# Both column halves of the first pointwise product walked in one pass over the depth, modulation units reordered

## The chip, the cores and the metric

The kernel runs on one core of one Trainium2 chip. The time is that of the device for one launch, in microseconds (us); the median of three runs of the kernel before is 1011.45 us (1011.24 to 1011.48).

## What is computed

Two transformer-like blocks run one after the other on 256 tokens of width 1024, in fp32. The change lies wholly in the first half of the first block:

```
mod  = silu(c) @ w_mod + b_mod                 # six vectors of 1024: scale1, shift1, gate1, scale2, shift2, gate2
hl   = rms_norm(x, norm1_g) * (1 + scale1) + shift1
u    = hl @ w_pw1 + b_pw1                      # 1024 -> 2048: halves a and gate
u    = a * sigmoid(gate)
u    = depthwise_conv(u, width 31, segments of 64) + b_dw
u    = silu(layer_norm(u))
x    = x + gate1 * (u @ w_pw2 + b_pw2)
x    = x + gate2 * (relu((rms_norm(x, norm2_g) * (1 + scale2) + shift2) @ mlp_w1) ** 2 @ mlp_w2)
```

What follows (attention of three kinds, a gated MLP, an embedding gate, twice) isn't touched.

## The kernel before

**Weights as a stream.** All weights lie in HBM in the order in which they are used, cut into units of 1 MB (128 partitions x 2048 floats). `plan_units` (L85) writes this order out by hand. SyncE (SP) issues one DMA for each unit, in that order (`weights`, L508). In the first block a unit goes to the slot "its index modulo 6" (L166, `EARLY_SLOTS`), and its DMA waits until whoever reads the unit six places earlier has finished with it: for a split unit until its low part is made (`lo_done`), for a modulation unit until VectorE's dot products (`dot_done`) or TensorE's products (`mod_used`) are done. All of SP's work is one queue in program order, the small transfers among it.

**Split units.** A product in full precision takes three fp32r passes: ScalarE (ACT) copies a weight unit to its high part (`feed` of ACT, L626, at L635), VectorE (DVE) subtracts to get the low part (`feed` of DVE, L1087, at L1101), and TensorE (PE) does high x high, high x low and low x high (`three`, L1707, at L1713). There are three buffers for split parts; the high part of unit s waits until PE has done unit s-3 (`used`).

**The first pointwise product (pw1).** 1024 inputs are four depth groups of 256 (`GROUPS`, two k-tiles of 128 each); 2048 outputs are two column halves c = 0, 1, each for 512 columns of a and 512 of gate. So pw1 is eight units, named (c, i) here. `pw1_part` (L1841) does one k-tile or two of one unit for one token block b: 6 matmuls a k-tile, 24 a unit with both blocks. PE does all of c = 0 first, in four groups, and c = 1 behind it (L1917 to L1952). Before group i its input must be scaled and shifted by modulation: the scale columns come from a dot product on DVE (`dots`, L1161, two instructions a unit), the shift columns from PE (`quarters`, L1810, 8 matmuls and then `column_sums`, L1822, with a copy by ACT between, `quarter_copy`, L688). `group_input` (L1204) on DVE and `group_high` (L699) on ACT make the full, high and low parts of the input.

**Modulation units.** mod(v, q) is quarter q of vector v: v = 0 scale1, 1 shift1, 2 gate1, 3 shift2, 4 scale2, 5 gate2. Those in `DOTS` (L82) go to DVE, at 2 x 1024 elements a unit; the eight others go to PE. The units before, by index: mod00, pw1(0,0), mod10, then mod0i, mod1i, pw1(0,i) for i = 1 to 3, pw1(1,0) to (1,2), mod20, pw1(1,3), pw2(0), mod21, mod22, pw2(1), mod23, mod40, mod30, mod41, mod31, mod42, pw2(2), mod32, pw2(3), mod43, mod33.

**The convolution.** It is done as a product with fixed waves: `gates` (ACT, sigmoid, L707), `gated` (DVE, L1246), `modes` (PE, L1866), `filtered` (DVE, L1252), `tokens` (PE, L1874), `statistics` and `variance` (DVE), a small power on GpSimd, then ACT and DVE normalise one token block each (L749, L1308), `normal_T` (PE, L1886) transposes, `pair_of` (ACT, L757) applies silu and `low_pair` (DVE, L1313) makes the low part.

**Second pointwise product and residual.** pw2 is four units. DVE has the low parts of pw2(2) and pw2(3), dot products between them, and then `mid_residual` (L1343), which needs gate1 in rows: `gate_column(0)` (DVE, L1283) makes it from the dot products of mod20 to mod23, SP writes it to HBM (`gate_write`, L540, waits for `gate_done`) and reads it back broadcast (`gate_read`, L545). In SP's order:

```python
            end = units_of("pw2")[2]["index"]
            weights(UNITS[at:end])
            gate_write(0)
            at, end = end, units_of("pw2")[3]["index"] + 1
            weights(UNITS[at:end])
            gate_read(0, one["g1"])
```

In ACT's order of the kernel before, the high parts of pw2(0) and pw2(1) stand ahead of the sigmoids of c = 1 (L741 to L743), and a one-element Silu (L745) loads the next activation table.

Of the kernel before, what the change touches and what calls it, by code (L numbers as in the profile page):

```python
# [41 lines left out]
HD = 5  # L42
# [39 lines left out]
DOTS = {(0, 0), (0, 1), (0, 2), (0, 3), (2, 0), (2, 1), (2, 2), (2, 3), (4, 2), (3, 2), (4, 3), (3, 3), (5, 0), (5, 1), (5, 2), (5, 3)}  # L82


def plan_units():  # L85
# [34 lines left out]
    mod(2, 1, 2)  # L120
    pw2(1)
    mod(2, 3)
    mod(4, 0)
    mod(3, 0)
    mod(4, 1)
    mod(3, 1)
# [60 lines left out]
LOW_IN_TWO = [u["s"] for u in SPLIT if (u["stage"][0], u["n"], u["part"]) in (("mla", 0, 1), ("sb", 0, 0), ("gu", 0, 1), ("gate", 0, 3))]  # L187

MOD_BANKS = [5] * GROUPS + [7, 6, 2, 3]
SUM_AT = [(6, 0)] * GROUPS + [(3, QUARTER)] + [(6, 0)]  # L190
COLUMN_UNITS = ((None, 0), (None, 1), (None, 2), (None, 3), (4, 5), (6, 7))
# [46 lines left out]
def build(nc, stream, x, p_t, vectors, rows, rel, consts, dft_tables, taps, tap_bias, out):  # L238

    ctx = ExitStack()  # L240
    with ctx:
# [146 lines left out]
        names = """used mod_used hi_done lo_done lo_first norm_half in_ident in_consts in_vec in_x0 in_x1 in_rows in_tables in_gain in_lora in_p  # L388
# [34 lines left out]
        def stage_free(eng, m):  # L423

            if m < 4:
                return
            eng.wait_ge(S["col_sums"], [m - 4 in g for g in COLUMN_UNITS].index(True) + 1)
# [79 lines left out]
        def _(sp):  # L507
# [53 lines left out]
            weights(UNITS[EARLY_SLOTS:10])  # L561
# [3 lines left out]
            weights(UNITS[10:at])  # L565
# [57 lines left out]
        def _(act):  # L623
            fed = [0]

            def feed(unit, ahead=LOOKAHEAD):  # L626

                while fed[0] < min(unit["s"] + 1 + ahead, len(SPLIT)):
# [6 lines left out]
                    nc.scalar.activation(hi[:, u["s"] % SPLIT_SLOTS, 0:n], raw_of(u, n),  # L635
# [52 lines left out]
            def quarter_copy(m):  # L688

                act.wait_ge(S["mod_used"], copies(m))  # L690
                stage_free(act, m)
                nc.scalar.activation(stage[:, m % 4, :], ps[:, MOD_BANKS[m], 0:QUARTER], ACT.Copy).then_inc(S["quarter_sb"], 1)

            def wave_copy(c):

                act.wait_ge(S["wave_ps"], c + 1)
                nc.scalar.activation(wc[0:MODES, c * CHUNK:(c + 1) * CHUNK], ps[0:MODES, 7, :], ACT.Copy).then_inc(S["wave_done"], 1)
# [9 lines left out]
            def gates(c):  # L707
                for b in range(NB):
# [13 lines left out]
            feed(units_of(("pw1", 0))[0], 0)  # L722
            quarter_copy(0)
            group_high(0)
            for i in range(1, GROUPS):
                quarter_copy(i)
                feed(units_of(("pw1", 0))[i], 0)
                if i == 2:
                    act.wait_ge(S["rel_ps"], 1)
                    nc.scalar.activation(rel_row, ps[0:HD, 7, 0:HOT], ACT.Copy).then_inc(S["toep_done"], 1)  # L730
                if i == 3:
                    wave_copy(0)
# [12 lines left out]
            nc.scalar.activation(one["warm"], vec[:, V_LNB:V_LNB + 1], ACT.Silu)  # L745
            quarter_copy(4)
# [4 lines left out]
            quarter_copy(5)  # L751
# [15 lines left out]
            for i in range(KT // 2):  # L767
                pair_of(i, ACT.Silu, vec[:, V_LNG:V_LNG + KT], vec[:, V_LNB:V_LNB + KT], "silu_done", "yh_done")
                if i < 2:
                    quarter_copy(6 + i)  # L770
# [313 lines left out]
        def _(dve):  # L1084
            fed = [0]

            def feed(unit, ahead=LOOKAHEAD, after_first=None):  # L1087

                while fed[0] < min(unit["s"] + 1 + ahead, len(SPLIT)):
# [4 lines left out]
                    dve.wait_ge(S["hi_done"], u["s"] + 1)  # L1094
                    first = u["cols"] if u["s"] in LOW_IN_TWO else 0
                    if first:
                        nc.vector.tensor_tensor(lo[:, slot, 0:first], raw_of(u, n)[:, 0:first], hi[:, slot, 0:first].bitcast(F32),
                                                ALU.subtract).then_inc(S["lo_first"], 1)
                        if after_first:
                            after_first()  # L1100
                    nc.vector.tensor_tensor(lo[:, slot, first:n], raw_of(u, n)[:, first:n], hi[:, slot, first:n].bitcast(F32),  # L1101
# [69 lines left out]
            def scale_columns(g):  # L1171
# [7 lines left out]
                else:  # L1179
                    dve.wait_ge(S["col_sums"], g + 1)  # L1180
# [8 lines left out]
            def shift_columns(g):  # L1189
# [7 lines left out]
                else:  # L1197
                    dve.wait_ge(S["col_sums"], g + 1)
# [5 lines left out]
            def group_input(i):  # L1204
                ks = slice(GROUP_KT * i, GROUP_KT * (i + 1))
                if i == 0:
                    dve.wait_ge(S["csb_done"], 2)
                    dve.wait_ge(S["xnT_ready"], 1)
                dots(0, i)
                scale_columns(i)  # L1210
                if i == 0:
                    dve.wait_ge(S["xnT_ready"], 1 + NB)
                    feed(units_of(("pw1", 0))[i], 0)
                shift_columns(i)
                dve.wait_ge(S["scale_done"], i + 1)
                dve.wait_ge(S["shift_done"], i + 1)
                for k in range(GROUP_KT):
                    kk = ks.start + k
# [1398 lines left out]
```

## Time and profile before

| | |
|---|---|
| median of 3 runs | 1011.45 us |
| profiled execution, span | 1008.9 us |
| time outside the span | 2.55 us |
| PE busy | 982.8 us (97%) |
| DVE busy | 625.9 us (62%) |
| ACT busy | 501.2 us (50%) |

The span runs from the first instruction to the last of one profiled execution; the time of a run is some 2.5 us longer. An engine's busy time is the sum of its instructions; since matmuls overlap in the pipeline, a stretch in which PE shows 100% is one without gaps, not one at the peak. The chain that ended last tells which engine's work, step by step, set the end. The part that the change touches is the first 122 us.

### The profile page before, as it was taken

How to read it: one execution, taken by the hardware profiler on the slowest of the kernel's cores; microseconds unless marked ns; L12 is line 12 of the kernel's file. 1: busy time of each engine (PE TensorE's matmuls, PEld its weight loads, DVE VectorE, ACT ScalarE, POOL GpSimd, SP SyncE). 2: the span in 40 equal slices, each digit the busy share in tenths (PEclk: the TensorE clock that was granted, in tenths of full speed). 3: DMA queues.
4: the chain of work that ended last, by engine and by line, in shares of the span. 5: the costliest groups of instructions: out<-in, count | busy, mean ns of one | idle time of the engine just before them, and what ended most of it. 6: DMA issues, size and time to landing. Idle time of an engine off the chain costs nothing.

```text
span 1008.9 us, 13430 instructions
## 1 busy us (share of the span) xinstructions
PE 982.8 (97%) x5588; PEld 833.9 (83%) x5588; DVE 625.9 (62%) x766; ACT 501.2 (50%) x628; POOL 29.4 (3%) x49
## 2 busy tenths in 40 slices
PE   7999999999999999999999999999999999999996
PEld 6665899999988998878888888889987888888885
DVE  5777866564457569765454545763987655555565
ACT  4445465445445447654444344653565544444453
POOL 0000100000002000010000000010000100000010
PEclk9999999999999999999999999999999999999999
DMA  9979747676342633345555556445324455455521
GB/s 336 418 300 351 308 162 278 258 281 253 136 156 112 241 103 120 123 159 209 190 186 189 186 193 216 143 150 188 128 82 168 161 208 204 172 204 172 203 105 42
DMA packets 31222, 196.60 MB, mean 195 GB/s; under 512 B 3891, under 2 KB 5992, under 8 KB 10168
## 3 DMA queue, kind: packets, MB, share of 16 engines
q1 hardware_dynamic: 31162, 195.75, 52.7%
q8 instruction: 44, 0.72, 0.3%
q14 instruction: 16, 0.13, 0.0%
HBM read 194.67 MB, written 2.05 MB: 195 GB/s over the span
## 4 chain that ended last, share of the span: by engine, by line
PE 81%; DVE 11%; issue 3%; DMA 2%; ACT 2%; SPq 0%; POOL 0%; DVEq 0%; POOLq 0%; ACTq 0%
PE ps L1713 59%; PE ps L2069 8%; PE ps L2137 5%; DVE lo L1101 3%; DMA scratch<-stream 2%; ACT hi L635 1%; PE ps L2391 1%; PE ps L2273 1%; DVE scratch L1511 1%; PE ps L1799 1%; PE ps L2164 1%; DVE scratch L1571 1%; DVE scratch L1528 1%; PE ps L1818 0%; PE ps L2294 0%
## 5 line engine op out<-in xcount | busy, mean ns | idle before, releaser
L1101 DVE TENSOR_TENSOR lo<-raw,hi 128x2048 fp32r<-128x2048 f32 (+6 forms) x139 | 309.1, 2227 | 223.8 <-ACT hi L635 223.7
L635 ACT ACTIVATE hi<-raw 128x2048 fp32r<-128x2048 f32 (+3 forms) x139 | 262.0, 1889 | 140.8 <-PE ps L1713 120.7
L1713 PE MATMUL ps<-hi,xh 128*128 128x512 f32 (+2 forms) x708 | 277.9, 393 | 6.3 <-DVE lo L1101 3.1
L1713 PE MATMUL ps<-lo,xh 128*128 128x512 f32 (+2 forms) x708 | 272.2, 384 | 0.0
L1713 PE MATMUL ps<-hi,xl 128*128 128x512 f32 (+2 forms) x708 | 271.9, 384 | 0.0
L1713 PEld LDWEIGHTS ps<-hi,xh 128*128 128x128 f32 x708 | 133.5, 189 | 40.7 <-issue 7.8
L1713 PEld LDWEIGHTS ps<-lo,xh 128*128 128x128 f32 x708 | 133.4, 188 | 25.6
L1713 PEld LDWEIGHTS ps<-hi,xl 128*128 128x128 f32 x708 | 133.5, 189 | 23.1
L1713 PE MATMUL ps<-hi,gh 128*128 128x512 f32 (+2 forms) x308 | 118.5, 385 | 0.0
L1713 PE MATMUL ps<-lo,gh 128*128 128x512 f32 (+2 forms) x308 | 118.1, 384 | 0.0
L1713 PE MATMUL ps<-hi,gl 128*128 128x512 f32 (+2 forms) x308 | 118.1, 383 | 0.0
L1713 PEld LDWEIGHTS ps<-lo,gh 128*128 128x128 f32 x308 | 57.9, 188 | 11.4
L1713 PEld LDWEIGHTS ps<-hi,gh 128*128 128x128 f32 x308 | 57.9, 188 | 10.9
L1713 PEld LDWEIGHTS ps<-hi,gl 128*128 128x128 f32 x308 | 57.9, 188 | 10.8
L2069 PE MATMUL ps<-xh,hi 128*128 128x256 f32 x224 | 63.4, 283 | 0.0
L2069 PE MATMUL ps<-xh,lo 128*128 128x256 f32 x224 | 63.4, 283 | 0.0
L2069 PE MATMUL ps<-xl,hi 128*128 128x256 f32 x224 | 63.4, 283 | 0.0
L2137 PE MATMUL ps<-xh,hi 128*128 128x256 f32 x192 | 55.2, 288 | 0.7 <-DVE lo L1101 0.7
L2137 PE MATMUL ps<-xl,hi 128*128 128x256 f32 x192 | 54.3, 283 | 0.0
L2137 PE MATMUL ps<-xh,lo 128*128 128x256 f32 x192 | 54.3, 283 | 0.0
L975 ACT ACTIVATE scratch<-ps,rstd 128x256 f32<-128x256 f32 x44 | 20.8, 473 | 55.3 <-PE ps L1713 55.3
L991 ACT ACTIVATE gh<-ps 128x256 fp32r<-128x256 f32 x40 | 13.2, 382 | 65.9 <-PE ps L2391 65.9
(275 smaller groups left out, 1161.6 us busy)
## 6 DMA issues: line engine op xcount, KB each, us to landing
raw<-stream SPq DMA_DIRECT2D x142, 1024.0 KB, 4.8
scratch<-stream SPq DMA_DIRECT2D x22, 1024.0 KB, 7.3
raw<-stream SPq DMA_DIRECT2D x4, 1020.0 KB, 4.8
raw<-stream SPq DMA_DIRECT2D x4, 896.0 KB, 5.6
raw<-stream SPq DMA_DIRECT2D x2, 864.0 KB, 4.5
raw<-stream SPq DMA_DIRECT2D x2, 768.0 KB, 4.2
raw<-stream SPq DMA_DIRECT2D x2, 680.0 KB, 6.0
h<-x SPq DMA_DIRECT2D x2, 512.0 KB, 4.7
```

The source lines that it names most:

```text
L635: nc.scalar.activation(hi[:, u["s"] % SPLIT_SLOTS, 0:n], raw_of(u, n), ACT.Copy).then_inc(S["hi_done"], 1)
L975: nc.scalar.activation(silu2[:, b, :], ps[:, gate_bank(j, b), 0:FF_CHUNK], ACT.Silu, scale=scale).then_inc(S["silu_g"], 1)
L991: nc.scalar.activation(dst[:, 0:2, b * P:(b + 1) * P], ps[:, 6 + b, 0:2 * P].rearrange("p (k m) -> p k m", k=2), ACT.Copy).then_inc(S["gh_ ...
L1101: nc.vector.tensor_tensor(lo[:, slot, first:n], raw_of(u, n)[:, first:n], hi[:, slot, first:n].bitcast(F32), ALU.subtract).then_inc(S["lo_ ...
L1511: nc.vector.scalar_tensor_tensor(out=work[b], in0=r[:, k, :], scalar=iw[:, b, head:head + 1], in1=in1, op0=ALU.mult, op1=ALU.add).then_inc ...
L1528: nc.vector.match_replace(work[b], top8[:, b, :], work[b], TAKEN).then_inc(S["topk_step"], 1)
L1571: nc.vector.tensor_scalar(pm[b][:, hh, :], pm[b][:, hh, :], row_inv[:, c:c + 1], None, ALU.mult).then_inc(S["m_norm"], 1)
L1713: ins = nc.tensor.matmul(out, l, r, start=start and i == 0, stop=stop and i == 2, skip_group_check=skip)
L1799: ins = nc.tensor.transpose(ps[:, 4 + 2 * b + k // 4, (k % 4) * P:(k % 4 + 1) * P], xs[:, b, k * P:(k + 1) * P], ident)
L2069: ins = nc.tensor.matmul(out_, w[:, k, cs], a[:, kk, :], start=(kk == 0 and c % 2 == 0 and i == 0), stop=(kk == KT - 1 and i == 2), skip_g ...
L2137: ins = nc.tensor.matmul(ps[:, bank + c // 2, (c % 2) * SEQ:(c % 2 + 1) * SEQ], w[:, k, cs], a[:, kk, :], start=(kk == 0 and c % 2 == 0 an ...
L2164: nc.tensor.matmul(ps[:, t_ // 2, (t_ % 2) * SEQ:(t_ % 2 + 1) * SEQ], w[:, k, cs], a[:, k0 + k, :], start=(k == 0 and t_ % 2 == 0 and i == ...
```

## The change

The stream's new order, by index: mod0i, mod1i, pw1(0,i), pw1(1,i) for i = 0 to 3 (indices 0 to 15), then 16 mod20, 17 mod21, 18 mod40, 19 mod30, 20 pw2(0), 21 mod41, 22 mod31, 23 mod22, 24 pw2(1), 25 mod23, 26 mod42, 27 pw2(2), 28 mod32, 29 pw2(3), 30 mod43, 31 mod33. Three shift units (mod11, mod12, mod13) go from PE to DVE's dot products, so five units are left for PE: mod10 at the start, and mod40, mod30, mod41, mod31, which PE now does in a row behind the last `tokens`. The full input of groups 1 to 3 is made by ACT (`group_full`) instead of DVE. The four units pw1(0,i) are split in two halves, so that PE can begin with the first. The table of waves and the relative bias move behind unit (0,0). `gate_column(0)` and the three mask copies move down in DVE's order, and the high part of pw2(1) moves behind the sigmoids in ACT's.

```diff
-DOTS = {(0, 0), (0, 1), ... }
+DOTS = {(1, 1), (1, 2), (1, 3), (0, 0), (0, 1), ... }
...
-    mod(0, 0)
-    pw1(0, 0)
-    mod(1, 0)
-    for i in range(1, GROUPS):
+    for i in range(GROUPS):
         mod(0, i)
         mod(1, i)
         pw1(0, i)
-    for i in range(3):
         pw1(1, i)
-    mod(2, 0)
-    pw1(1, 3)
+    mod(2, 0, 1)
+    mod(4, 0)
+    mod(3, 0)
     pw2(0)
-    mod(2, 1, 2)
+    mod(4, 1)
+    mod(3, 1)
+    mod(2, 2)
     pw2(1)
     mod(2, 3)
-    mod(4, 0)
-    mod(3, 0)
-    mod(4, 1)
-    mod(3, 1)
     mod(4, 2)
...
@@ SyncE
-            sp.dma_start(stack_rows, rows["stack"]).then_inc(S["in_rows"], 16)
-            weights(UNITS[0:EARLY_SLOTS])
+            at = units_of(("pw1", 1))[0]["index"] + 1
+            weights(UNITS[0:at])
+            sp.dma_start(stack_rows, rows["stack"]).then_inc(S["in_rows"], 16)
...
@@ ScalarE
+            def quarter_pair(m):
+
+                act.wait_ge(S["mod_used"], copies(m + 1))
+                if stage_of(m + 1) == stage_of(0):
+                    act.wait_ge(S["col_sums"], 1)
+                at = stage_of(m)
+                nc.scalar.activation(stage[:, at:at + 2, :].rearrange("p i c -> p (i c)"), ps[:, MOD_AT[m][0], :],
+                                     ACT.Copy).then_inc(S["quarter_sb"], 1)
...
+            def group_full(i):
+
+                act.wait_ge(S["xg_lo"], i)
+                for k in range(GROUP_KT):
+                    kk = GROUP_KT * i + k
+                    nc.scalar.activation(xf[:, k, :], xnT[:, kk, :], ACT.Identity, scale=in_scale[:, kk:kk + 1],
+                                         bias=in_shift[:, kk:kk + 1]).then_inc(S["xf_done"], 1)
...
             for i in range(1, GROUPS):
-                quarter_copy(i)
                 feed(units_of(("pw1", 0))[i], 0)
...
                 group_high(i)
-            feed(units_of(("pw1", 1))[0], 0)
-            wave_copy(1)
-            feed(units_of(("pw1", 1))[1], 0)
+                group_full(i)
+                feed(units_of(("pw1", 1))[i], 0)
 
             act.wait_ge(S["pick_done"], 2)
-            gates(0)
-            feed(units_of(("pw1", 1))[3], 0)
+            gates(0, 0, 1)
             feed(units_of("pw2")[0], 0)
+            gates(1, 0, 1)
             feed(units_of("pw2")[1], 0)
-            gates(1)
 
             nc.scalar.activation(one["warm"], vec[:, V_LNB:V_LNB + 1], ACT.Silu)
-            quarter_copy(4)
+            quarter_pair(1)
...
-            quarter_copy(5)
+            quarter_pair(3)
...
@@ VectorE
+            def group_input(i):
+
+                dots(0, i)
+                scale_columns(i)
+                dots(1, i)
+                shift_columns(i)
+                feed(units_of(("pw1", 0))[i], 0)
+                group_low(i)
+                feed(units_of(("pw1", 1))[i], 0)
...
-            gated(0, 0, 1)
-            feed(units_of(("pw1", 1))[2], 0)
             dots(2, 0)
-            feed(units_of(("pw1", 1))[3], 0)
+            gated(0, 0)
+            dots(2, 1, 0)
+            gated(0, 1)
+            dots(2, 1, 1)
             dve.wait_ge(S["wave_done"], CHUNKS)
-            filtered(0, 0, 1, 2, 3)
-            dots(2, 1)
+            filtered(0, 0, 1)
+            gated(1, 0)
+            filtered(0, 2, 3)
             feed(units_of("pw2")[0], 0)
+            gated(1, 1)
             statistics(0, 0)
             statistics(0, 1)
-            dots(2, 2)
-            dots(2, 3)
+            filtered(1, 0, 1, 2, 3)
+            statistics(1, 0)
+            variance(0)
+            statistics(1, 1)
+            variance(1)
+            dots(2, 2, 0)
...
-            gate_column(0)
...
-            gated(1, 0)
-            feed(units_of("pw2")[1], 0)
-            gated(1, 1)
-            filtered(1, 0, 1, 2, 3)
...
-            scale_columns(4)
-            shift_columns(4)
+            dots(2, 2, 1)
+            for g in (4, 5):
+                scale_columns(g)
+                shift_columns(g)
...
             for i in range(KT // 2):
                 low_pair(i, "yh_done", "yl_done")
-                if i < 2:
-                    dots(4, 2, i)
-            scale_columns(5)
-            shift_columns(5)
+            feed(units_of("pw2")[1], 0)
+            dots(2, 3)
+            gate_column(0)
+            dots(4, 2)
             feed(units_of("pw2")[2], 0)
...
@@ TensorE
             for i in range(GROUPS):
...
+                if i == 0:
+                    pw1_part(0, 0, 0, (0,))
+                    pw1_part(0, 0, 1, (0,))
+                    pw1_part(0, 0, 0, (1,))
+                    used(pw1_part(0, 0, 1, (1,)), None)
...
+                    waves(0)
+                    waves(1)
...
+                else:
+                    group(0, i, 0)
+                    group(0, i, 1)
+                group(1, i, 0)
...
+                if i == GROUPS - 1:
+                    modes(0, 0)
+                    modes(0, 1)
+                group(1, i, 1)
             pe.wait_ge(S["in_consts"], 32)
             tokens(0, 0)
+            modes(1, 0)
             tokens(0, 1)
...
             modes(1, 1)
             tokens(1, 0)
             tokens(1, 1)
-            quarters(4)
-            quarters(5)
+            pe.wait_ge(S["modes_done"], SEGS * CHUNKS)
+            for m in range(1, len(MODS)):
+                quarters(m)
             normal_T(0)
-            pe.wait_ge(S["quarter_sb"], copies(5))
             normal_T(1)
             column_sums(4)
-            quarters(6)
-            pe.wait_ge(S["shift_done"], 5)
-            quarters(7)
+            column_sums(5)
```

## Rows read from the trace of the kernel before

**Rows 1.** The page: busy time, and the chain that ended last by engine.

```profile
PE 982.8 (97%) x5588; PEld 833.9 (83%) x5588; DVE 625.9 (62%) x766; ACT 501.2 (50%) x628; POOL 29.4 (3%) x49
...
PE 81%; DVE 11%; issue 3%; DMA 2%; ACT 2%; SPq 0%; POOL 0%; DVEq 0%; POOLq 0%; ACTq 0%
```

**Rows 2.** Chain in order of time, first 122 us: start, length (us), what.

```profile
5.68 19.52 DMA scratch<-stream
...
43.34 1.04 PE ps L1883 x2
...
50.34 0.66 PE ps L1860 x2
...
55.65 5.66 PE ps L1713 x24
61.31 1.91 PE ps L1871 x8
...
87.34 1.08 PE ps L1878 x4
88.42 1.04 PE ps L1818 x16
...
91.02 1.96 PE ps L1890 x16
...
96.30 2.95 PE ps L1713 x12
...
110.79 4.59 DVE raw L1168 x8
...
116.13 0.70 DVE xs L1352
```

**Rows 3.** TensorE in order of time, its first matmul of pw1: start, length, line, tile.

```profile
21.13 0.53 PE L1713 MATMUL ps<-hi,xh 128*128 128x512 f32 x1
```

**Rows 4.** Stages: busy time, PEclk (granted clock), DMA share, GB/s, by stretch.

```profile
8.00:16.00 8.00, 4.24 (x38) 3.56 (x42) 4.71 (x9) 5.64 (x6) 0.74 (x2) 1.00 1.01 419
18.00:20.00 2.00, 2.00 (x11) 2.00 (x11) 1.44 (x5) 1.09 (x2) 0.00 (x0) 0.50 0.98 406
20.00:22.00 2.00, 2.00 (x11) 1.86 (x11) 1.94 (x4) 0.00 (x0) 0.00 (x0) 0.70 1.04 422
30.00:40.00 10.00, 9.51 (x51) 6.43 (x52) 7.75 (x15) 3.65 (x5) 0.00 (x0) 1.00 1.02 416
```

**Rows 5.** VectorE in order of time, columns as in rows 3, idle time last.

```profile
84.71 2.58 DVE L1258 TENSOR_TENSOR scratch<-ps,scratch 120x512 f32<-120x512 f32 x4
...
100.25 0.69 DVE L1316 TENSOR_TENSOR xl<-scratch,xh 128x512 fp32r<-128x512 f32 x1 [0.88 <-ACT xh L763]
...
104.01 2.28 DVE L1101 TENSOR_TENSOR lo<-raw,hi 128x2048 fp32r<-128x2048 f32 x1
```

**Rows 6.** ScalarE in order of time, columns as in rows 5.

```profile
76.56 1.92 ACT L635 ACTIVATE hi<-raw 128x2048 fp32r<-128x2048 f32 x1 [5.67 <-PE ps L1713]
...
83.47 0.60 ACT L713 ACTIVATE scratch<-ps 128x512 f32<-128x512 f32 x1 [3.00 <-PE ps L1860]
84.08 1.28 ACT L745 ACT_TABLE_LOAD   x1
...
89.77 1.20 ACT L749 ACTIVATE xs<-ps,scratch 128x1024 f32<-128x1024 f32 x1
...
98.55 1.00 ACT L759 ACTIVATE scratch<-ps,scratch 128x256 f32<-128x256 f32 x2
99.58 0.63 ACT L763 ACTIVATE xh<-scratch 128x512 fp32r<-128x512 f32 x1
```

**Rows 7.** A lone 1 MB transfer, issued at 83.42: last column us to landing.

```profile
raw<-stream SPq DMA_DIRECT2D x1, 1024.0 KB, 4.8
```

**Rows 8.** SyncE in order of time, gate write and the weights behind it.

```profile
83.79 0.43 SPq L543 DMA_DIRECT2D gate_dram<-scratch  x1
84.27 0.43 SPq L522 DMA_DIRECT2D raw<-stream  x1
```

More of the change, by code:

```diff
@@ L186 @@
 DOT_UNITS = [u for u in UNITS if "d" in u]
[L187 to L191, printed above, removed]
+LOW_IN_TWO = [u["s"] for u in SPLIT if u["stage"] == ("pw1", 0) or (u["stage"][0], u["n"], u["part"]) in (("mla", 0, 1), ("sb", 0, 0), ("gu", 0, 1), ("gate", 0, 3))]
+FRONT_PAIRS = [u["s"] for u in SPLIT if u["stage"] == ("pw1", 0)]
+MOD_AT = [(5, 0), (6, 0), (6, QUARTER), (7, 0), (7, QUARTER)]
+SUM_GROUPS = (0, GROUPS, GROUPS + 1)
+SUM_AT = {0: (6, 0), GROUPS: (2, 0), GROUPS + 1: (3, 0)}
+COLUMN_UNITS = {0: (None, 0), GROUPS: (1, 2), GROUPS + 1: (3, 4)}
 WARM = (8, 6, 7, 8)
@@ L420, in build, with stage_of @@
         SB_GROUPS = ((slice(0, 3), slice(5, 8)), (slice(3, 5), slice(0, 2)))
[L423 to L427, printed above, removed]
+        def stage_of(m):
+            return (m - 1) % 4
         NORMS = 3 + 3 * LAYERS + 1
@@ L560, in _ @@
             sp.dma_start(padded_taps, taps).then_inc(S["in_tables"], 16)
-            weights(UNITS[EARLY_SLOTS:10])
+            end = last_of(("pw1", 1))["index"] + 1
+            weights(UNITS[at:end])
             sp.dma_start(table[:, P:C_HOT], consts[:, P:C_HOT]).then_inc(S["in_consts"], 16)
@@ L564, in _ @@
             at = units_of("pw2")[1]["index"]
-            weights(UNITS[10:at])
+            weights(UNITS[end:at])
             sp.wait_ge(S["toep_done"], 1)
@@ L1179, in scale_columns @@
                 else:
[L1180 removed]
+                    dve.wait_ge(S["col_sums"], SUM_GROUPS.index(g) + 1)
                     bank, at = SUM_AT[g]
@@ L1202, in shift_columns, with group_low @@
                                         ALU.add).then_inc(S["shift_done"], 1)
-            def group_input(i):
+            def group_low(i):
                 ks = slice(GROUP_KT * i, GROUP_KT * (i + 1))
[L1206 to L1218, printed above, removed]
-                    nc.vector.tensor_scalar(xf[:, k, :], xnT[:, kk, :], in_scale[:, kk:kk + 1], in_shift[:, kk:kk + 1],
-                                            ALU.mult, ALU.add).then_inc(S["xf_done"], 1)
-                if i:
-                    feed(units_of(("pw1", 0))[i], 0)
                 dve.wait_ge(S["xf_done"], GROUP_KT * (i + 1))
@@ L1238, in bias_rows @@
                 nc.vector.tensor_tensor(pick, first_ones, second_ones, ALU.add).then_inc(S["pick_done"], 1)
-            for i in range(GROUPS):
+            first_group()
+            for i in range(1, GROUPS):
                 group_input(i)
-                if i == 0:
-                    bias_rows()
-            feed(units_of(("pw1", 1))[1], 0)
             def gated(c, *blocks):
@@ L1331, in _ @@
                 shift_columns(g)
+            dve.wait_ge(S["in_consts"], 32)
+            for dst, c in ((ident16[:], C_ID), (masks16[:, 0, :], C_CAUSAL), (masks16[:, 1, :], C_STRICT)):
+                nc.vector.tensor_copy(dst, table[:, c:c + P]).then_inc(S["masks_done"], 1)
             rstep = [0]
@@ L1836, in column_sums @@
                         at = first + GROUP_KT * v + k
-                        ins = nc.tensor.matmul(ps[:, bank, at:at + 1], stage[:, m % 4, k * P:(k + 1) * P], one["sel1"],
+                        ins = nc.tensor.matmul(ps[:, bank, at:at + 1], stage[:, stage_of(m), k * P:(k + 1) * P], one["sel1"],
                                                start=True, stop=True)
```

131 lines of the change are left out of this document (64 added, 67 removed).

## The prediction

> **What bounds the kernel now.** Read first the page [rows 1]: TensorE (PE) is busy 97% of the span, and the chain that ended last runs 81% through it. That is a mean over stages. So read next the chain in order of time [rows 2], and stage by stage ask who is late. In the first 44 us it is the weight stream: the chain waits 19.5 us for units to land, and the DMA share from 30 to 40 us is full, at 416 GB/s [rows 4]; that is 1.05 MB each 2.52 us. From 44 to 83 us it is PE without a gap, 5.66 us a unit. From 83 to 93 us it is a chain of short steps (sigmoid, product, `modes`, `filtered`, `tokens`, normalise, transposes), from 93 to 116 us pw2, with VectorE (DVE) last: it makes low parts and dot products without a pause until 115.4 [rows 2], and the residual begins at 116.13. Behind that PE is the bound again, so what the residual's start moves, the end moves.
>
> **How the two times stand.** I work with the profiled execution (span 1008.9); the median is 1011.45, 2.55 more, and I carry that over: predicted median = 1011.45 + shift of the residual's start.
>
> **Part 1, the front: a gain.** Today three units must land for each 5.66 us of PE work in c = 0, at 7.6 us, and c = 1 comes behind. New, four units (10.1 us) bring two PE units (11.3 us), so PE is the bound as soon as it starts. Start: mod10 now lands second, so its product comes right behind the warming matmuls; the two halves of pw1(0,0) let PE start when the first low part is there. I get 20.4 instead of 21.1 [rows 3]. Then eight units x 5.66 = 45.3; bias rows 4 x 0.66 = 2.6; bias table and two waves, about 0.8 + 2 x 1.04 = 2.9; the first half's `modes` 1.9 [rows 2]; waits for group 1 and 2 about 0.7. Sum 20.4 + 53.4 = 73.8. The old sigmoid behind the last pw1 matmul starts at 83.47 [rows 6], the new one at 73.9: 9.6 earlier.
>
> Does DVE keep up? A group has four dot-product instructions at 1.15 (110.79, x4 pairs in 4.59 [rows 2]), two low parts at 2.2 [rows 5], the input's low part 0.6 and some 0.6 of small columns: 10.2 of the 11.3 us. The full input goes to ScalarE (ACT), 1.0 a group beside two high parts at 1.9 [rows 6]; nobody waits for that. Slots: the unit six places back is always freed in time here. The three shift units that move to DVE cost 6.9 us of DVE, hidden by PE. If that cover were gone, they would cost up to that.
>
> **Part 2, to the end of the last `tokens`.** Old: 83.47 to 88.42, 4.95 us [rows 2, 6]. New, DVE has the low part of pw2(0), then the sigmoid product, then two `statistics` that wait for `tokens(0,1)` ahead of the four `filtered` (2.58 [rows 5]): sigmoid at 73.9; its product at 75.3 (DVE has the low part until 74.6); `statistics` until 77.4 (the second waits for `tokens(0,1)` at 76.7); `filtered` 79.9; `tokens` done at 81.0 (1.08 [rows 2]). Gain left: 88.4 - 81.0 = 7.4.
>
> **Part 3, ScalarE waits for a weight unit: a loss.** pw2(1) is index 24, and takes the slot of index 18, mod40. mod40 used to be elsewhere; now PE multiplies it behind the last `tokens`, so SyncE (SP) can issue pw2(1) only at 81.0 + 1.04 (eight matmuls, as in [rows 2] at 88.42). ACT's program has the high part of pw2(1) ahead of the Silu table, of `quarter_pair(1)` and of the normalisation of block 0. So all of that waits: issue 82.05, landing + 4.8 [rows 7] = 86.9, high part 1.9 -> 88.8, table load 1.28 and one-element Silu 0.2 -> 90.3, pair copy 0.5 -> 90.8, normalise 1.2 -> 92.0 [rows 6], 16 transposes 1.96 [rows 2] -> 94.0. Today they end at 92.98. So the front's gain is spent at this point, and 1.0 us more. Without that wait the transposes would begin when PE is through with its four units, at 81.0 + 4.2 = 85.2, and end at 87.2.
>
> While it waits, PE has nothing from 85.2 to 92.0. In this trace PE, busy 4.2 of the 8 us up to 16.0, was granted 0.50 (1.2 GHz of 2.4) from 18 to 20 and 0.70 on the mean from 20 to 22 [rows 4]. After 6.8 us of nothing I expect the same, and the transposes take 1.96 more at half speed; bounds 0 and 2.0, and I take 1.7: end at 95.7.
>
> The Trainium skill ("ScalarE: Activation LUTs", What ACT_TABLE_LOAD costs) gives 2.66 us for a switch, 1.28 of load and 1.38 of drain, which speaks against putting a switch behind a late unit. By it the shift would be 1.4 us larger; the load here stands 0.01 us behind the sigmoid [rows 6], so the drain isn't seen, and the trace doesn't agree.
>
> **Part 4, the gate write holds back the stream: a loss.** SP's order is unchanged: weights up to index 26, then `gate_write(0)`, then 27 pw2(2), 28, 29, the gate read, 30, 31. `gate_write` waits for `gate_column(0)`, which today DVE makes ahead of the sigmoid products of c = 1; SP comes to the write at 83.79 and has the next weights out 0.48 later [rows 8]. New, it comes behind the four low parts, the low part of pw2(1) and the last two dot products of gate1. From the transposes' end: four pairs of ACT at about 1.6 [rows 6] = 6.4, low part 0.6 [rows 5], low part of pw2(1) 2.25, dots(2,3) 2.3, column 0.2: 11.75, so 107.45 with part 3's slow clock. Queued behind on SP are pw2(2), mod32, pw2(3), mod43 and mod33, none of which has been issued. SP writes (0.45 [rows 8]), then issues pw2(2), which lands 4.75 later at 112.65; mod32, pw2(3), the 0.5 MB gate read, mod43 and mod33 follow at 2.5 each and 1.3: the last lands at 112.65 + 11.3 = 124.0. Dot products on it 2.3, columns 0.75, mask copies 0.45: DVE comes to the residual at 127.5. PE: high and low part of pw2(2) 4.2 -> 116.9, two units 11.3 -> 128.2 (some 1.5 more if its clock falls again). The last quarter of the residual isn't due before 131.5, so PE has slack and DVE, behind the stream, is last.
>
> **Sum.** 127.5 - 116.13 = 11.4. Further on, w1(0)'s units, due at 127 to 130, delay the square of block 0 on ACT by some 0.2. Shift +11.6, or, from the terms: -9.6 (front), +2.2 (longer convolution chain), +8.4 (ACT behind pw2(1)), +1.7 (clock), +8.7 (pw2 stage: 31.8 from the transposes' end to the residual, against 23.15), +0.2. Median 1011.45 + 11.6 = 1023.0.
>
> The Trainium skill ("DMA: Bandwidth & Descriptors", Anatomy of one DMA) says that DMA engines do not wait on semaphores: the wait is on the issuing sequencer. By it the write's wait stops everything behind it on SP, as part 4 has it; were it only in the write's own ring, part 4 would cost nothing and the first rival would hold. The trace of before has no gate wait to show which.
>
> **The rivals.**
> A. Only the first stall holds: the units behind the gate write get out in time (SP runs past its wait, or `gate_done` is earlier than I have it). For it: in this trace the write costs SP 0.43 us and no more [rows 8]. Against: one program order. DVE would then run without a pause behind the four low pairs: 95.7 + 7.0 + three low parts 6.75 + five dot units 11.5 + columns and masks 1.2 = 122.15, 6.0 behind today; with the 0.2 below it 1017.7.
> B. Neither stall bites, the result is faster. One mechanism: pw2(1)'s slot is free before PE's four products (if its predecessor were done elsewhere), so that ACT never waits, and the gate column is early enough. Then the transposes end at 87.2 and DVE runs through as in A: 87.2 + 26.45 = 113.65, residual 2.5 earlier: 1009.0. It decides from the point at which pw2(1) is issued by 75 (4.8 + 1.9 + 1.5 before `quarter_pair(1)` is due at 83). Against it stands the rule "index modulo 6": 24 and 18 share slot 0.
> C. The front gives less: DVE or a landing stalls PE in each group, 10.2 of 11.3 us being tight. At 1 us more in groups 1 to 3, everything moves by 3: 1026.
> D. The clock doesn't fall: 1021.3. This is inside the main case.
>
> **How the numbers follow.** Two tenths of a per cent (2 us) is about what a measurement of this kernel can tell from no change. Main case (with D) 0.78, its own range 1019 to 1026; A 0.08; C 0.05; B 0.06; gains of the same kind that leave it within 2 us 0.03. Slower by over 0.2%: 0.78 + 0.08 + 0.05 = 0.91; same 0.03; faster 0.06. The range reaches down to A and up to C: 1016 to 1026.5.
>
> **What would show it.** In the trace of after: PE with hardly a gap from 20.4 to 74 us (front right; gaps of over 1 us before each pw1(0,i) would be C). ACT idle for some 12 us ahead of a high part, released by a DMA, from 74.5 to 86.9, and PE idle before its transposes on ACT's normalised block; if the transposes end before 90, part 3 is wrong. SP's gate write at about 107 with the next weight DMA behind it, the DMA share near nothing from 95 to 107; if weights are issued between, part 4 is wrong. The granted clock between 86 and 96: 0.5 to 0.7, or 1.0 (D). The residual's first instruction at 125.5 to 128. The prediction fails as a whole if later stages, which I take to be bound by PE, give time back.

## The result, and the profile after

The changed kernel takes 1025.23 us (median of 4, 1024.78 to 1026.52) beside 1011.35 us for the kernel before (median of 4; the prediction had 1011.45, of 3): 1.0138 times as long, 95% interval 1.0126 to 1.015, or 13.9 us more. 11.6 had been predicted, 1023.0, in the range 1016.0 to 1026.5. The profiled execution is the slowest of the four (1026.52, span 1024.4, 15.5 more than the span of before), so what its rows show sums to some 1.5 us more than the medians do.

The page of the kernel after, busy time and the chain that ended last; it stands against [rows 1]:

```profile
PE 987.1 (96%) x5528; PEld 839.0 (82%) x5528; DVE 631.0 (62%) x776; ACT 503.1 (49%) x633; POOL 31.5 (3%) x49
...
PE 80%; DVE 10%; ACT 3%; DMA 3%; issue 2%; POOL 1%; DVEq 0%; SPq 0%; POOLq 0%; ACTq 0%
```

Nothing there tells that the kernel is slower, or where: every share is within a point or so. The chain in order of time does (start, length, what), beside [rows 2]:

```profile
21.87 5.73 PE ps L1741 x24
...
30.25 31.95 PE ps L1741 x132
...
82.75 1.05 PE ps L1846 x16
...
83.81 4.83 DMA raw<-stream
...
90.59 1.28 ACT L760
...
93.72 3.69 PE ps L1917 x16
...
104.55 2.20 DVE lo L1119
...
109.27 0.33 SPq L539
...
109.64 5.02 DMA raw<-stream
...
118.95 12.38 DMA raw<-stream
...
131.35 1.91 ACT hi L637
...
136.42 1.63 PE ps L2023 x8
138.06 2.89 PE ps L1925 x16
140.95 2.75 PE ps L1741 x12
```

The 19.5 us of waiting for the stream at the start ([rows 2]) are gone; in their place three transfers stand in the chain, at 83.81, 109.64 and 118.95, in a stage that had none. The first is a weight that ScalarE waits for. ScalarE in order of time (start, length, line, operation, tiles; in brackets the idle time ahead and what ended it), beside [rows 6]:

```profile
75.45 0.60 ACT L731 ACTIVATE scratch<-ps 128x512 f32<-128x512 f32 x1 [4.77 <-PE ps L1887]
88.67 1.91 ACT L637 ACTIVATE hi<-raw 128x2048 fp32r<-128x2048 f32 x1 [12.62 <-DMA raw<-stream]
90.59 1.28 ACT L760 ACT_TABLE_LOAD   x1
91.89 0.20 ACT L760 ACTIVATE scratch<-scratch 128x1 f32<-128x1 f32 x1
```

The second hangs on SyncE's queue, in order of time, beside [rows 8]:

```profile
83.81 1.67 SPq L518 DMA_DIRECT2D raw<-stream  x3
109.27 0.33 SPq L539 DMA_DIRECT2D gate_dram<-scratch  x1
109.64 0.43 SPq L518 DMA_DIRECT2D raw<-stream  x1
```

For 24 us no weight is issued, then the next 0.37 us behind the start of the gate write. Stretches of after (columns as in [rows 4]: after busy times the granted clock, DMA share and GB/s):

```profile
88.00:90.00 2.00, 0.00 (x0) 0.00 (x0) 0.00 (x0) 1.33 (x1) 0.00 (x0) 0.76 1.00 422
90.00:92.00 2.00, 0.00 (x0) 0.00 (x0) 0.00 (x0) 1.97 (x4) 0.00 (x0) 0.50 1.02 430
...
96.00:98.00 2.00, 2.00 (x12) 2.00 (x10) 0.00 (x0) 0.56 (x2) 0.00 (x0) 0.50 0.00 0
...
106.00:108.00 2.00, 2.00 (x8) 1.12 (x8) 2.00 (x4) 0.00 (x0) 0.00 (x0) 0.97 0.03 8
...
120.00:122.00 2.00, 2.00 (x6) 1.52 (x6) 1.59 (x5) 1.59 (x1) 0.00 (x0) 0.50 0.98 377
```

The engines that carry the weights move next to nothing from 94 to 110 us, and TensorE is granted 1.2 GHz (0.50) from 90 to 106. Stage by stage, the time from one place to the next, as after minus before:

| | predicted | measured |
|---|---|---|
| to the last sigmoid of pw1 (83.47 before, 75.45 after) | -9.6 | -8.0 |
| from there to the last `tokens` (88.42, 82.75) | +2.2 | +2.35 |
| to the end of the transposes (92.98, 97.41) | +10.1 | +10.1 |
| to the residual's first instruction (116.13, 129.78) | +8.7 | +9.2 |
| to the first hidden unit behind it (125.27, 140.95) | +0.2 | +2.0 |
| sum | +11.6 | +15.7 |

### The profile page after: what moved, and what is told of

It is laid out like the page before. It is cut to its first block, busy times and chain, and to the rows that moved or that the text cites. A ratio compares the mean times of both kernels' runs of the same rounds, so it can differ in the third digit from the quotient of the medians.

```text
span 1024.4 us, 13309 instructions
## 1 busy us (share of the span) xinstructions
PE 987.1 (96%) x5528; PEld 839.0 (82%) x5528; DVE 631.0 (62%) x776; ACT 503.1 (49%) x633; POOL 31.5 (3%) x49
## 4 chain that ended last, share of the span: by engine, by line
PE 80%; DVE 10%; ACT 3%; DMA 3%; issue 2%; POOL 1%; DVEq 0%; SPq 0%; POOLq 0%; ACTq 0%
PE ps L1741 58%; PE ps L2093 8%; PE ps L2161 5%; DMA raw<-stream 3%; DVE lo L1119 3%; ACT hi L637 1%; PE ps L2415 1%; PE ps L2297 1%; DVE scratch L1539 1%; PE ps L1925 1%; PE ps L2188 1%; DVE scratch L1599 1%; PE ps L1827 1%; DVE scratch L1556 1%; PE ps L2318 0%
## 5 line engine op out<-in xcount | busy, mean ns | idle before, releaser
L1119 DVE TENSOR_TENSOR lo<-raw,hi 128x2048 fp32r<-128x2048 f32 (+5 forms) x141 | 310.5, 2205 | 224.5 <-ACT hi L637 224.4
L637 ACT ACTIVATE hi<-raw 128x2048 fp32r<-128x2048 f32 (+6 forms) x141 | 263.1, 1870 | 157.9 <-PE ps L1741 108.0
L1741 PEld LDWEIGHTS ps<-lo,gh 128*128 128x128 f32 x308 | 57.9, 188 | 11.3
```

What stands on the lines that cost most here:

```text
L637: nc.scalar.activation(hi[:, u["s"] % SPLIT_SLOTS, first:n], raw_of(u, n)[:, first:n], ACT.Copy).then_inc(S["hi_done"], 1)
L1741: ins = nc.tensor.matmul(out, l, r, start=start and i == 0, stop=stop and i == 2, skip_group_check=skip)
```

## The experiments

Each kernel is timed beside the kernel before on the same chip, whose median lay between 1011.16 and 1011.42 there. Two changed kernels are compared by their medians across chips. "Later" and "earlier" are of profiled executions, one for each kernel.

**ScalarE's order alone.** The high part of pw2(1) goes behind the four silu pairs.

```diff
             gates(1, 0, 1)
-            feed(units_of("pw2")[1], 0)
...
                 pair_of(i, ACT.Silu, ...)
+            feed(units_of("pw2")[1], 0)
             feed(units_of("pw2")[2], 0)
```

> The changed kernel with one move in ScalarE's order: the high part of pw2(1) stands behind the four silu pairs instead of ahead of the Silu table. Theory (ScalarE waits for pw2(1) ahead of the normalisation): the transposes begin when TensorE is through with its four modulation units, at about 87.0, and end at about 89.0 instead of 97.4; TensorE's clock stays at 1.0 there. The low part of pw2(1) then ends at 99.5 instead of 106.7, the gate write and all behind it come 7.2 us earlier, the residual begins at about 122.6, and the time is 1018.0 us (1.0066 of before). Rival (the four modulation units on TensorE, or the longer convolution chain, are what holds the normalisation): the transposes still end behind 95 and the time stays at about 1025.

Measured: 1017.07 (4 executions, 1015.76 to 1019.1), 0.9 below the theory's number, ratio 1.0056, interval 1.0039 to 1.0073. Chain of this kernel:

```profile
85.48 1.98 PE ps L1917 x16
...
100.53 0.33 SPq L539
...
100.90 5.46 DMA raw<-stream
```

The transposes end at 87.46, 10 us earlier than in the changed kernel, and at full clock; the gate write comes 8.7 earlier, the median is 8.2 lower. TensorE hadn't been kept from the transposes by its own four products, but by ScalarE's wait. The second stall is still there: the next weight leaves 0.37 behind the start of the gate write.

**SyncE's order alone.** pw2(2), mod32, pw2(3) go ahead of the gate write, mod43 and mod33 ahead of the gate read.

```diff
-            end = units_of("pw2")[2]["index"]
+            end = units_of("pw2")[3]["index"] + 1
             weights(UNITS[at:end])
             gate_write(0)
-            at, end = end, units_of("pw2")[3]["index"] + 1
+            at, end = end, units_of("w1", 0)[0]["index"]
```

> The changed kernel with one move in SyncE's order: the weights pw2(2), mod32 and pw2(3) are issued ahead of the gate write, mod43 and mod33 ahead of the gate read. Theory (the gate write holds the stream back): weights are issued between 95 and 107 us, the high part of pw2(2) begins at 103.8 instead of 114.7, VectorE runs through, the residual begins at about 123.9 instead of 129.8, the units of w1(0) are there in time (1.4 us more), and the time is about 1017.7 us (1.0063). The transposes still end at 97.4. Rival (VectorE's own work, 7 us of dot products more than before, sets the residual): the residual stays within 1 us of 129.8, and so does the time within 1 us of 1025.2.

Measured: 1017.92 (1017.04 to 1018.38), as the theory has it (1017.7), ratio 1.0061, interval 1.0046 to 1.0076. SyncE in order of time:

```profile
82.90 2.32 SPq L518 DMA_DIRECT2D raw<-stream  x4
...
85.49 1.94 SPq L518 DMA_DIRECT2D scratch<-stream  x2
...
108.24 0.33 SPq L539 DMA_DIRECT2D gate_dram<-scratch  x1
```

The write is as late as ever, but six weight transfers are out by 87.4. They leave even earlier than the theory had it (95 to 107). VectorE then works without a gap from 102.8 to the residual at 122.86, 6.9 earlier than in the changed kernel; the median is 7.3 lower. So the waiting write held back everything behind it on its queue. (By "DMA: Bandwidth & Descriptors" of the Trainium skill, Anatomy of one DMA, the semaphore wait is the issuing sequencer's; both kernels' traces agree, with the weight issued at 109.64 in one and from 82.90 in the other.)

**Both orders.**

> Both moves at once (high part of pw2(1) behind the silu pairs, gate write behind pw2(3)). Theory (both stalls, and behind them VectorE alone): low pairs end at 95.9, and from there three low parts, five dot units and 1.2 us of small work: the residual begins at 116.5 to 117, 0.4 to 0.9 us later than before, and the time is 1011.5 to 1012.5 us (1.000 to 1.001): the 8 us that the front gains are used up by VectorE's idle time between the low pairs. Rival (the two stalls are all that is lost): the front's gain comes out, residual at 113 to 114, time 1008 to 1009.

Measured: 1010.6 (10 executions, 1009.49 to 1012.98), ratio 0.9994, interval 0.9985 to 1.0004: no difference from the kernel before, and between what the two sides expected. Chain:

```profile
19.79 7.33 PE ps L1741 x24
...
85.77 1.98 PE ps L1917 x16
...
109.76 4.58 DVE raw L1186 x8
...
121.47 1.09 PE ps L2023 x8
122.56 3.18 PE ps L1925 x16
125.74 2.97 PE ps L1741 x12
```

The two mended orders give 14.6 us, nearly the sum of 8.2 and 7.3: the stalls are two, and add up. What is left of the front's gain is small: 8.7 us at the last sigmoid (74.79 against 83.47) are 6.3 at the last `tokens`, 5.2 at the end of the transposes and 0.7 at the residual (115.44). The trace shows where they go. The convolution chain is longer, as predicted. VectorE is last throughout pw2 (its last dot products from 109.76), and has stood still for 3.5 us in all between the four low pairs and the low part of pw2(1) before that. Behind the residual the 16 dummy instructions took 3.18 instead of 1.79, with the clock at 0.67 and 0.50. And the front itself was slower than in the changed kernel, since the first unit of pw1 took 7.33 us instead of 5.73, with the clock at 0.57.

**TensorE kept at work ahead of the transposes** (changed kernel, 28 dummy matmuls behind the modulation products).

```diff
                 quarters(m)
+            for _ in range(28):
+                nc.tensor.matmul(ps[:, 4, 0:P], neg_ones[:], neg_ones[:], start=True, stop=True)
             normal_T(0)
```

> The changed kernel with 28 dummy 128-column matmuls on TensorE between its four modulation units and the transposes, some 7 us of work in the time in which it waits for ScalarE. Theory (the clock at 1.2 GHz costs the transposes 1.7 to 1.9 us on the chain): the granted clock stays at 1.0 from 86 to 106 us, the 16 transposes take 1.96 instead of 3.7 us, everything behind comes 1.7 to 1.9 us earlier, time about 1023.4 us. Rival (the clock only lengthens work that has slack): time unchanged within 0.5 us of 1025.2. Second rival (the whole stretch at the low clock, 88 to 106 us, is lost): 6 us or more earlier, 1019.

Measured: 1025.48 (1023.25 to 1026.15), ratio 1.0133, interval 1.0118 to 1.0148: no gain to be seen, though the step itself did what it should. Steps of the chain, and a wait of TensorE (us in total, times, longest):

```profile
93.14 1.98 PE ps L1917 x16
...
116.67 13.67 DMA raw<-stream
...
135.06 1.97 PE ps L2025 x8
```

```profile
PE ps L2025 <- DVE xs L1393: 4.0, 1, 4.0
```

The transposes take 1.98 instead of 3.69, the gate write comes 2.3 earlier, and so does the residual (127.39 against 129.78; counted from the last `tokens` 2.0). So the slow transposes were on the path that far. What takes the gain back stands behind: the unit of w1(0) that the square waits for lands 13.67 behind its issue instead of 12.38, so the normalised residual is only 1.4 earlier, and there TensorE has stood still for 4.0 us (2.9 in the changed kernel) and the clock fell. The transposes and the dummies behind them took 5.3 us, 4.5 in the changed kernel, 2.9 at full clock. The first hidden unit is 0.6 earlier, 0.2 counted from the last `tokens`.

**And ahead of the residual's transposes too** (the kernel above, with `keep_busy(30)` and `keep_busy(22)` for `keep_busy(8)` there).

> The changed kernel with 28 dummy matmuls ahead of its transposes of pw2's input (as in e4_busy_28), and 30 instead of 8 dummy matmuls ahead of the residual's first transposes (`mid_T(0)`). In e4_busy_28 TensorE stood still for 4.0 us there, the clock fell to 0.50, and the eight transposes with the 16 dummies behind them took 5.30 us against 2.88 at full clock. The 22 more take 2.4 us, inside the 4.0. Theory (the 1.7 us of slow transposes were a real term, and the fall of the clock at the residual has hidden the gain of taking it away): transposes 1.09 and dummies 1.79, first hidden unit at about 138, median 2.4 below e4_busy_28, 1023.0. Rival (what was gained ahead goes into the queue of the stream, whose last unit for the square landed only 1.0 earlier, and the clock falls there whatever TensorE does in between): 1025 to 1025.5.

Measured: 1025.61 (1023.91 to 1026.42), ratio 1.0143, interval 1.0127 to 1.0158: next to the rival's number. The clock stayed and the first hidden unit starts at 137.82, as the theory has it, and this execution is the fastest of the four. But the dummies took 6.70, more than was free, since one is two instructions of 0.11, so the next kernel has fewer.

> As e9_busy_28_30, with 22 instead of 30 dummy matmuls ahead of the residual's first transposes. One dummy matmul is two instructions and takes 0.223 us (30 took 6.70 us in e9_busy_28_30), so 30 were longer than the time TensorE had free there and made its transposes 1.3 us late; 22 take 4.9 us of the 5.8 that were free in e4_busy_28. Theory (the clock's fall behind the late square is what hides the gain of the faster transposes ahead): first hidden unit at 137.2 or before, 3 us earlier than in e4_busy_28 (140.37), median 1022.5 to 1023.5. Rival (something behind the first hidden unit takes it back, or the executions scatter by more than the gain, as the four of e9_busy_28_30 do from 1023.9 to 1026.4): 1025 to 1025.5.

Measured: 1024.78 (1024.03 to 1025.7), ratio 1.013, interval 1.0115 to 1.0146. The clock at the residual stays at 1.00 and the dummies behind its transposes take 1.79. Chain, and one stretch of 2 us:

```profile
116.64 13.97 PE ps L1741 x48
130.61 4.91 PE ps L1925 x44
135.52 0.87 PE ps L2025 x8
```

```profile
118.00:120.00 2.00, 2.00 (x6) 1.53 (x5) 1.58 (x3) 1.26 (x1) 0.00 (x0) 0.50 1.06 430
```

The first hidden unit starts at 138.29, 2.1 earlier than with 28 dummies alone (the theory had 3), and the median lies just below the rival's range. TensorE stands still from 111.4 to 116.6, waiting for pw2(2) behind the gate write, and then does the last two units at 0.50 until 122: 13.97 us instead of the 11.3 of two units at full clock. Now TensorE is last at the residual. So keeping the clock at one gap doesn't keep it at the next, as long as that gap is there.

What the 1.7 us of slow transposes were worth at the end isn't settled by these three kernels. Counted from the last `tokens`, the first hidden unit comes 0.2, 1.4 and 2.0 us earlier than in the changed kernel. Their twelve executions average 1025.1 us, the four of the changed kernel 1025.4, and each kernel's own executions lie 1.7 to 2.9 us apart. (In the last profile 1.3 us are lost far behind: from the first hidden unit to the end it takes 885.2 us, in the other thirteen profiles 883.4 to 884.3.)

**Both orders, and more dummies ahead of the residual's transposes** (`keep_busy(30)`, then `keep_busy(20)`).

> e3_both (both orders mended) with 30 instead of 8 dummy matmuls ahead of the residual's first transposes. In e3_both the residual starts 0.7 us earlier than in the kernel before, yet the first hidden unit starts 0.5 us later: the 16 dummies behind the transposes take 3.18 us instead of 1.79, with the clock at 0.67 and 0.50, behind 3.2 us in which TensorE stood still. Theory: with the idle time filled up to 0.8 us the clock stays, first hidden unit at 124.3, median 1.4 below e3_both: 1009.2, faster than before by 0.2%. Rival (the fall isn't due to that idle time): dummies 3.2 us again, 1010.6.

Measured: 1011.66 (11 executions, 1010.42 to 1012.28), ratio 1.0001, interval 0.9993 to 1.001: too many dummies here as well. Their 6.70 us made the transposes start at 123.04, 1.6 later, and what they saved behind was 1.4.

> As e10_both_busy_30, with 20 instead of 30 dummy matmuls ahead of the residual's first transposes: 4.5 us of the 5.0 that TensorE had free in e3_both; 30 took 6.7 and made the transposes 1.6 us late, at full clock. Theory: transposes at 121.5 and the dummies behind them 1.79 instead of 3.18, first hidden unit at 124.3, 1.4 earlier than in e3_both: median 1009.2 to 1009.7. Rival (no difference, the fall of the clock there isn't what the time hangs on): 1010.6 to 1011.

Measured: 1010.31 (11 executions, 1008.93 to 1011.47), ratio 0.9986, interval 0.9978 to 0.9995. Chain:

```profile
120.92 1.09 PE ps L2023 x8
122.02 1.79 PE ps L1925 x16
123.91 3.01 PE ps L1741 x12
```

In the profiled execution the first hidden unit starts 1.8 earlier than with eight (125.74), 1.4 of it by dummies at full clock, as the theory has it; the medians differ by 0.3, short of the 0.9 to 1.4 expected. The profiled execution of the kernel with eight had been 1.0 above its own median. Perhaps the clock doesn't fall there in all its executions; only one was profiled, so that isn't shown.

**Gaps of VectorE filled** (both orders, and:)

```diff
                 pair_of(i, ACT.Silu, ...)
-            feed(units_of("pw2")[1], 0)
+                if i == 1:
+                    feed(units_of("pw2")[1], 0)
...
                 low_pair(i, "yh_done", "yl_done")
-            feed(units_of("pw2")[1], 0)
-            dots(2, 3)
-            gate_column(0)
+                if i < 2:
+                    dots(2, 3, i)
+                if i == 1:
+                    feed(units_of("pw2")[1], 0)
+                    gate_column(0)
```

> Both moves of the run before, and VectorE's idle time between the low pairs filled: the two dot products of mod23 behind the first two low pairs, then the low part of pw2(1) and the gate column, ahead of the last two low pairs; ScalarE makes the high part of pw2(1) behind its second silu pair. Theory (with both stalls gone, VectorE's idle time between the low pairs eats the front's gain): the residual begins at about 112 instead of 115.4, the last matmul of pw2 is at 113.7, and the time is about 1007.3 us (0.996 of before). Rival (something else, TensorE's products of pw2 or the landing of mod33, sets the residual): less than 1 us against 1010.6.

Measured: 1007.61 (5 executions, 1005.91 to 1008.42), ratio 0.9956, interval 0.9943 to 0.9968. Chain:

```profile
84.28 1.97 PE ps L1920 x16
...
101.11 10.75 DMA raw<-stream
...
111.88 1.92 ACT hi L637
```

3.0 faster than with the two orders alone, and now faster than the kernel before. The median is what was expected. In the profiled execution the residual starts at 109.96, 2 us before the expected place and 5.5 earlier than with both orders. Of these, 1.5 are already there at the last sigmoid (73.30 against 74.79), where the clock fell once instead of twice; the other 4.0 come behind it, where the gaps were filled. The span is 5.7 shorter, and the medians differ by only 3.0, since one profiled execution is 1.7 below its median and the other 1.0 above. The chain no longer runs through the residual, but through a w1 unit that was issued at 101.11 and whose high part stands ahead of the square of block 0 on ScalarE; that costs some 0.8 us (the normalised residual 6.1 behind the residual, 5.3 in the kernel with both orders).

**Was the front bound by VectorE?** (both orders; the dot products of mod11 to mod13 go over 8 elements instead of 1024, so these shift columns lack the rest of their sums.)

> Both moves, and the dot products of mod11, mod12 and mod13 (the three units that went from TensorE to VectorE) cut to 8 elements each, which leaves 6.9 us of VectorE's work in groups 1 to 3 and the right shift columns out of the computation. Theory (TensorE is the bound in the front, these dot products are hidden but for group 1): the last sigmoid of pw1 comes at most 1 us earlier than 74.75, time 1009.5 to 1010.6. Rival (VectorE bounds the groups, 10.2 of 11.3 us being too tight): the last sigmoid 3 us or more earlier, and the time 1007 to 1008.

Measured: 1010.23 (1008.42 to 1011.78), ratio 0.9986, interval 0.9977 to 0.9995; the last sigmoid of pw1 at 74.86, with whole dot products 74.79. So in these two executions the 6.9 us put on VectorE are hidden. In both, though, the clock fell twice in the front, which makes TensorE late. In the two profiles in which it didn't fall, TensorE waits for VectorE before groups 1 to 3, for 1.0 us in all, so up to that the dot products are not hidden; the medians, 0.4 apart, leave room for it.

**More dummies** (filled kernel, `keep_busy(20)` ahead of the residual's transposes; then 16 instead of 8 at the start as well).

> As the filled kernel, with 20 dummy matmuls instead of 8 on TensorE between pw2 and the transposes of the residual. Theory (the clock falls to 1.2 GHz in the idle time ahead of these transposes, and lengthens them and the dummy block behind them, on the path): the granted clock stays at 1.0 from 116 to 126 us, and the time is 1 to 1.5 us below the filled kernel. Rival (that stretch has slack, as the low clock at 88 to 106 us had): no change within 0.4 us.

> As the kernel with 20 dummy matmuls, and the dummy block ahead of pw1 16 matmuls long instead of 8. Theory (in the runs without it TensorE idles 1.8 us ahead of pw1, the clock then falls to 0.57 from 20 to 24 us, and the first unit takes 7.3 instead of 5.7 us): the first unit takes 5.7 us and everything behind comes about 1.3 us earlier, 1 to 1.5 us off the time. Rival (group 1 waits for VectorE and ScalarE anyway, so the first unit's speed is hidden): no change within 0.4 us.

Measured: 1007.1 (1006.45 to 1007.72), ratio 0.9954, interval 0.9942 to 0.9967, and 1007.1 (1006.32 to 1007.25), ratio 0.9951, interval 0.9939 to 0.9964. Neither differs from 1007.61. In the profile of the filled kernel the clock was 1.0 at both places already, so there was nothing for the dummies to save there, and they can't show what the clock costs. It had fallen from 28 to 32 us (0.59 and 0.55), and with 16 dummies at the start it didn't; but the last sigmoid came no earlier (73.54 against 73.30), since TensorE waited for VectorE instead. They stand as the lowest medians measured, 4.1 us below the kernel before.

## Why the prediction came out

**The front (right in length, 1.5 late; what sets it was read wrong).** From the first matmul of pw1 to the last sigmoid it had 53.5 us, measured 53.6 (21.87 to 75.45). It had VectorE busy 10.2 of the 11.3 us of a group, and said of ScalarE's work that nobody waits for it. But VectorE takes 11.5 us a group: it is stopped for 1.1 by ScalarE's high part of pw1(1,i), which stands behind the full input. One such wait, and the first matmul of group 3 in the changed kernel and in the one with 28 and 30 dummies:

```profile
48.72 2.29 DVE L1119 TENSOR_TENSOR lo<-scratch,hi 128x2048 fp32r<-128x2048 f32 x1 [1.12 <-ACT hi L637]
```

```profile
59.23 0.47 PE L1741 MATMUL ps<-hi,xh 128*128 128x512 f32 x1
```

```profile
57.53 0.47 PE L1741 MATMUL ps<-hi,xh 128*128 128x512 f32 x1 [0.34 <-DVE xl L1227]
```

Both stand 37.4 us behind their first matmul of pw1 (at 21.87 and 20.18). In the second, at full clock, TensorE waits three times, 1.0 us in all, where the prediction had 0.7 for two groups. In the first it shows no wait, but the clock is at 0.76 from 30 to 32 us and at 0.50 from 32 to 34, which costs TensorE 1.6 there and uses up the waits. So the third rival's mechanism, VectorE stopping TensorE in each group, is there, at a third of its price of 1 us a group.

The start is 21.87 instead of 20.4. That isn't a term of the change: in the profiled executions of the twelve kernels of the experiments it lies between 19.7 and 20.7. In the changed kernel's, one early product (L1931) took 3.78 us, in theirs 1.9 to 3.1. Each later place of the profiled execution up to the residual is 1.5 to 2.3 late against the prediction, most of it by this start.

**The convolution chain (right).** Sigmoid to `tokens`: 7.1 predicted, 7.3 measured.

**ScalarE behind pw2(1) (right in mechanism and size).** From the last `tokens` on: issue 1.05 later predicted, 1.06 measured; landing 4.8 and 4.83; transposes' end 14.7 and 14.66. Taking the one line out of ScalarE's order gave 8.2 us.

**The clock (right up to the residual, left out behind it).** 1.7 was predicted for the transposes, 3.69 - 1.98 = 1.71 is measured, and in the three kernels without this fall the residual comes 1.7 to 2.0 us earlier, counted from the last `tokens`. But the prediction put the second fall of the clock, at the residual, at nothing ("some 1.5 more" only for pw2's units, as slack), and it is there: 4.52 us for transposes and dummies instead of the 2.88 that they take at full clock. How much of the first fall reaches the end beside the second, and beside the late w1(0) unit, isn't shown (0.2 to 2.0 us at the first hidden unit, nothing to be told in the medians).

**The gate write (right).** From the transposes' end to the write 11.75 predicted, 11.86 measured; next landing 4.75 and 5.0; residual 20.05 and 20.5 behind the write. The first rival, that only ScalarE's stall holds, had worked out 1017.7 for the case that this one is absent; the kernel with SyncE's order mended is just that case, 1017.92. The second rival, neither stall, had 1009.0; with both mended 1010.6. It had the residual at 113.65, measured 115.44: in that kernel the high part of pw2(1) stands behind all four silu pairs, and VectorE can't begin its low part until 96.0.

**Behind the residual (mis-sized).** "Delay the square of block 0 by some 0.2", with w1(0)'s units due at 127 to 130. The second landed at 131.33, and its high part put the square off until 133.17, some 0.6 behind the residual rows that it needs. The normalised residual is 0.5 us later than the residual itself is (135.62 against 121.48 is +14.1, the residual +13.65), and the rest, 1.5, is the clock. So the term of 0.2 is 2.0 in the profiled execution, and this is the term of the sum that was mis-sized. The prediction is 4.1 short of this execution at the first hidden unit (1.6 in the front, 0.7 on the way to the residual, 1.8 here), and only 2.2 in the median: this execution is 1.3 above it. Its late start may be the reason; no other execution of this kernel was profiled.

The fourth rival, that the clock doesn't fall, goes with the stretches shown: 0.50 from 90 to 106.

What the prediction rests on behind all this, that the later stages give nothing back, holds: from the first hidden unit to the end it takes 883.6 us before and 883.5 after.

## What to carry over

When units of a stream are reordered, read every engine's program order again with the new index of each unit: a weight that lands late stops all that stands behind its consumer on an in-order engine, and a small transfer that waits for a result stops all weights behind it on its queue. Here the gain of 8 us in the front was real, and two lines that hadn't been moved with the stream cost 8 and 7 us; each is easy to find in the trace, as the longest idle time in front of one instruction and as an empty stretch of the DMA share. A fall of the clock that is taken away is worth only what the next idle time leaves of it: follow it, place by place, to the end of the sum.

## What was not expected of the hardware

Ahead of pw1 TensorE waits 1.83 us for the first low part, in every kernel with the new front but the one with 16 dummies there. In seven of the profiled executions the clock fell behind it (0.52 to 0.79 from 20 to 22 us) and the first unit took 7.3 to 7.4 us; in the five others with this wait it stayed, and the unit took 5.7 to 5.8. In eight of the thirteen it fell between 28 and 36 us, where TensorE shows no gap since its first matmul of pw1, and small products (bias table and waves) just before. What decides it isn't settled. What the falls cost depends on VectorE. The time from the first matmul of pw1 to the last sigmoid:

| falls of the clock in the front | profiled executions | us |
|---|---|---|
| none, or only the later one | 6, the changed kernel among them | 53.6 |
| only the first | 3 | 54.5 to 54.6 |
| both | 4 | 55.0 |

A single later fall costs nothing, since TensorE would have waited for VectorE. So 1.4 us can come and go between executions, and a part of the scatter may be this: the kernel before spans 1.8 us in the thirteen executions beside which the kernel with both orders spans 3.5 in ten.

Loading the activation table took 1.28 us in both kernels, and the next instruction of ScalarE started 0.02 behind its end (85.38 before, 91.89 after). The Trainium skill has a drain of 1.38 us beside the load ("ScalarE: Activation LUTs", What ACT_TABLE_LOAD costs); neither trace shows it.
